# Expert stage of a two-block transformer kernel: routing keys stored in pairs, row products respread, PSUM zeroed by ScalarE

## The reference

```python
def peer_ffn(h, w_q, sub_k1, sub_k2, expert_u, expert_v):
    q = (ht @ w_q).reshape(T, 8, 256)
    s1 = q[..., :128] @ sub_k1.T ; s2 = q[..., 128:] @ sub_k2.T      # T x 8 x 128 each
    v1, i1 = top_k(s1, 16) ; v2, i2 = top_k(s2, 16)
    vals, pos = top_k((v1[..., :, None] + v2[..., None, :]).reshape(T, 8, 256), 16)
    experts = take_along_axis(i1[..., None] * 128 + i2[..., None, :], pos)    # T x 8 x 16
    gates = softmax(vals)
    a = einsum('cd,chkd->chk', x, expert_u[experts])
    w = gelu(a) * gates
    return einsum('chk,chkd->cd', w, expert_v[experts])
```

## Time and profile before

| | us |
|---|---|
| runs: median (lowest, highest of 3) | 1773.2 (1770.69, 1775.11) |
| profiled execution, span from first to last instruction | 1771.5 |
| TensorE busy | 1735.8 |
| VectorE busy | 1119.2 |
| GpSimd busy | 301.4 |
| ScalarE busy | 240.8 |

### The profile page before, as it was taken

The page is one execution under the profiler, slowest core; times in us unless marked ns, Lnnn a source line. Parts: engine busy times, 40 slices in busy tenths (PEclk is TensorE's granted clock), DMA queues, the critical chain, the costliest instruction groups (busy, mean ns, idle before and its releaser), DMA issues.

```text
span 1771.5 us, 29553 instructions
## 1 busy us (share of the span) xinstructions
PE 1735.8 (98%) x11793; PEld 1482.8 (84%) x11793; DVE 1119.2 (63%) x2415; ACT 240.8 (14%) x599; POOL 301.4 (17%) x282
## 2 busy tenths in 40 slices
PE   8999999999999899999999999999999999999996
PEld 7898576986999899999999868699955978699942
DVE  4752432898657888799533533279974763379964
ACT  1014520110414111000000011111100001011100
POOL 0010000145433444444422200000000000000000
PEclk9999999999999999999999999999999999999998
DMA  7534234499999999999999844365554435354551
GB/s 276 190 122 164 72 119 143 155 337 372 414 416 416 405 407 398 373 412 415 415 417 418 344 202 160 126 223 172 171 173 166 167 121 191 117 170 167 170 182 50
DMA packets 76609, 439.62 MB, mean 248 GB/s; under 512 B 8566, under 2 KB 8656, under 8 KB 37840
## 3 DMA queue, kind: packets, MB, share of 16 engines
q1 hardware_dynamic: 42624, 305.15, 46.4%
q0 software_dynamic: 32592, 125.92, 18.3%
q10 hardware_dynamic: 1280, 6.95, 1.0%
HBM read 432.67 MB, written 5.24 MB: 247 GB/s over the span
## 4 chain that ended last, share of the span: by engine, by line
PE 81%; DMA 9%; DVE 8%; issue 1%; ACT 1%; POOL 0%; SPq 0%; POOLq 0%; DVEq 0%
PE ps L1139 16%; PE ps L921 14%; PE ps L540 10%; DMA arena<-u_rows,sparse_pairs 7%; PE ps L584 7%; PE ps L913 7%; PE ps L1177 4%; PE ps L623 3%; PE ps L498 3%; DVE arena L1912 2%; PE ps L776 2%; PE ps L823 2%; PE ps L789 1%; PE ps L934 1%; PE ps L1008 1%
## 5 line engine op out<-in xcount | busy, mean ns | idle before, releaser
L913 PE MATMUL ps<-xT,ring 128*128 128x150 f32 x2048 | 268.4, 293 | 0.0
L921 PE MATMUL ps<-arena,ring 128*128 128x150 f32 (+1 forms) x2048 | 266.3, 292 | 0.8 <-DMA ring<-stream 0.8
L913 PEld LDWEIGHTS ps<-xT,ring 128*128 128x128 f32 x2048 | 264.4, 191 | 0.1
L921 PEld LDWEIGHTS ps<-arena,ring 128*128 128x128 f32 x2048 | 262.3, 190 | 1.5 <-issue 1.5
L540 PE MATMUL ps<-ring,arena 128*128 128x512 f32 x416 | 181.4, 592 | 0.4 <-ACT arena L1487 0.4
L2033 DVE SCALAR_TENSOR_TENSOR arena<-arena,sparse_dots 128x1024 f32<-128x1024 f32 x105 | 134.7, 1283 | 73.4 <-DMA arena<-v_rows,sparse_pairs 68.2
L2501 POOL DMA_INDIRECT arena<-v_rows,sparse_pairs x107 | 132.8, 1241 | 224.9 <-DVE arena L2033 180.4
L1912 DVE CUSTOM_DVE_ANT_0 arena<-arena 128x1024 f32<-128x1024 f32 x107 | 127.9, 1223 | 66.9 <-DMA arena<-u_rows,sparse_pairs 66.3
L2501 POOL DMA_INDIRECT arena<-u_rows,sparse_pairs x107 | 132.4, 1238 | 167.9 <-DVE sparse_dots L1912 143.7
L2464 POOL TENSOR_SCALAR stat<-stat 128x1 f32<-128x1 f32 (+2 forms) x23 | 4.4, 190 | 913.8 <-DVE stat L2205 705.7
L540 PEld LDWEIGHTS ps<-ring,arena 128*128 128x128 f32 x416 | 78.0, 190 | 93.0 <-issue 92.3
(11 more groups left out here) (341 smaller groups left out, 2244.2 us busy)
## 6 DMA issues: line engine op xcount, KB each, us to landing
ring<-stream SPq DMA_DIRECT2D x288, 1024.0 KB, 7.5
arena<-second_params POOLq DMA_DIRECT2D x6, 1024.0 KB, 5.2
arena<-kv_scratch POOLq DMA_DIRECT2D x2, 2048.0 KB, 14.2
kv_scratch<-arena ACTq DMA_DIRECT2D x2, 1024.0 KB, 10.7
arena<-held_params ACTq DMA_DIRECT2D x1, 2048.0 KB, 16.5
arena<-u_rows,sparse_pairs POOLq DMA_INDIRECT x107, 13.7
arena<-v_rows,sparse_pairs POOLq DMA_INDIRECT x107, 11.2
arena<-second_params POOLq DMA_DIRECT2D x1, 1536.0 KB, 6.5
```

Of the source, the lines that this page charges most:

```text
L913: ins = pe.matmul(ps[:, o % 2, 0:DENSE], w[:, (o % 2) * D + k * P:(o % 2) * D + (k + 1) * P], xT[:, k, 0:DENSE], start=(k == 0), stop=(k = ...
L921: ins = pe.matmul(ps[:, 4 + k // 2, c:c + DENSE], w[:, (o % 2) * D + k * P:(o % 2) * D + (k + 1) * P], H[:, n, :], start=False, stop=last, ...
```

## The change

`sel16` holds each key and gate twice, side by side, so that the one-hots read them with an innermost run of two elements in place of a step of 0; the three one-hot instructions become four, `e_same` first, with one wait between. `DOTS_TURN` goes from 74 to 70, so that the turns are spread evenly from the first group on. The zeros in PSUM are no longer written by TensorE; ScalarE copies the zero tile into the four banks after its spill of the last keys, and TensorE waits for that (`sums_zeroed`) ahead of `mixed(1)`.

```diff
--- before.py
+++ after.py
@@ -54,7 +54,7 @@
 DOTS_SUMS = (4, 4, 4, 4, 3)
 DOTS_PICK = 3
 DOTS_FIRST = 70
-DOTS_TURN = 74
+DOTS_TURN = 70
 TURNS_UP = 116
 TURNS_DOWN = 164
 GATES_AT = 22
@@ -200,7 +200,7 @@
         stat = sb("stat", [P, 96])
         exps = sb("minus_half", [P, 16])
         mark_cell = sb("mark_cell", [P, 1])
-        sel16 = sb("sel16", [P, 4, DENSE], F16)
+        sel16 = sb("sel16", [P, 4, DENSE, 2], F16)
         e1 = sb("e1", [P, 2, 2, GROUP, HEAD], F16)
         e2 = sb("e2", [P, 2, GROUP, P], F16)
         e_same = sb("e_same", [P, 2, GROUP, HEAD], F16)
@@ -401,7 +401,7 @@
         iota_ready = sem("iota_ready")
         x_wide_ready = sem("x_wide_ready")
         dot_gelu_b, weight_b_ready = sem("dot_gelu_b"), sem("weight_b_ready")
-        zeros_ready = sem("zeros_ready")
+        zeros_ready, sums_zeroed = sem("zeros_ready"), sem("sums_zeroed")
         e_ready, gates_psum, gates_applied = sem("e_ready"), sem("gates_psum"), sem("gates_applied")
         expert_psum, expert_gelu = sem("expert_psum"), sem("expert_gelu")
         xres_T_psum, xres_T_ready = sem("xres_T_psum"), sem("xres_T_ready")
@@ -974,12 +974,8 @@
             mixed(0)
 
             pe.wait_ge(xres_T_ready, 4)
-            pe.wait_ge(zeros_ready, 1)
-            pe.wait_ge(xkv_ready, 16)
+            pe.wait_ge(sums_zeroed, 4)
             pe.wait_ge(gates_applied, GROUPS)
-            for b in range(4):
-                pe.matmul(ps[:, 4 + b, :], zeros[:], zeros[:].unsqueeze(1).to_broadcast([P, 4, P]),
-                          start=True, stop=False, skip_group_check=True)
             mixed(1)
 
             def down_turn(m, turns, last=False):
@@ -1414,6 +1410,11 @@
             act.dma_start(kv_scratch[0][:, K0_FIRST * 2 * T:KT * T],
                           yT[:, 0:KT - 2 * K0_FIRST, :].rearrange("p k t -> p (k t)")).then_inc(k0b_spilled, 16)
 
+            act.wait_ge(zeros_ready, 1)
+            for b in range(4):
+                act.copy(ps[:, 4 + b, :].rearrange("p (n c) -> p n c", n=4),
+                         zeros[:].unsqueeze(1).to_broadcast([P, 4, P])).then_inc(sums_zeroed, 1)
+
             def expert_act(n, b, m):
 
                 if b == 0:
@@ -2047,8 +2048,9 @@
             for n, i in enumerate(TILES):
                 dve.wait_ge(routed_psum, n + 1)
                 w = min(P, DENSE - i * P)
-                dve.tensor_copy(sel16[:, :, i * P:i * P + w],
-                                ps[:, 2 + n, :].rearrange("p (j t) -> p j t", j=4)[:, :, 0:w]).then_inc(sel_ready, 1)
+                dve.tensor_copy(sel16[:, :, i * P:i * P + w, :],
+                                ps[:, 2 + n, :].rearrange("p (j t) -> p j t", j=4)[:, :, 0:w].unsqueeze(3)
+                                .to_broadcast([P, 4, w, 2])).then_inc(sel_ready, 1)
             dve.wait_ge(sel_ready, 2)
             dve.wait_ge(iota_ready, 1)
 
@@ -2057,17 +2059,23 @@
                 if not first:
                     dve.wait_ge(gates_psum, q - 1)
 
-                def key(j, n):
-                    return sel16[:, j, group_at(g):group_at(g) + GROUP].unsqueeze(2).to_broadcast([P, GROUP, n])
+                def two(tile):
+                    return tile.rearrange("p t (m z) -> p t m z", z=2)
+
+                def of_token(j, n):
+                    return sel16[:, j, group_at(g):group_at(g) + GROUP, :].unsqueeze(2)\
+                        .to_broadcast([P, GROUP, n // 2, 2])
 
                 def numbers(a, n):
-                    return iota16[:, a:a + n].unsqueeze(1).to_broadcast([P, GROUP, n])
-
-                dve.tensor_tensor(e2[:, b], numbers(0, P), key(1, P), ALU.is_equal)
-                link(dve.tensor_tensor(e_same[:, b], numbers(hf * HEAD, HEAD), key(0, HEAD), ALU.is_equal))
-                gates_of = sel16[:, 2:4, group_at(g):group_at(g) + GROUP].unsqueeze(3).to_broadcast([P, 2, GROUP, HEAD])
-                dve.tensor_tensor(e1[:, b], e_same[:, b].unsqueeze(1).to_broadcast([P, 2, GROUP, HEAD]), gates_of,
-                                  ALU.mult).then_inc(e_ready, 1)
+                    return iota16[:, a:a + n].rearrange("p (m z) -> p m z", z=2).unsqueeze(1)\
+                        .to_broadcast([P, GROUP, n // 2, 2])
+
+                step.inc(dve.tensor_tensor(two(e_same[:, b]), numbers(hf * HEAD, HEAD), of_token(0, HEAD), ALU.is_equal))
+                dve.tensor_tensor(two(e2[:, b]), numbers(0, P), of_token(1, P), ALU.is_equal)
+                dve.wait_ge(dve_step, step.n)
+                for part in range(2):
+                    ins = dve.tensor_tensor(two(e1[:, b, part]), two(e_same[:, b]), of_token(2 + part, HEAD), ALU.mult)
+                ins.then_inc(e_ready, 1)
 
             def apply_gates(g, q, b, hf):
```

## The result

The changed kernel takes 1765.29 us (median; 1763.68 to 1767.05, 4 runs), the kernel before beside it 1773.68 (1770.69 to 1775.11, 4 runs): a ratio of 0.9949, 95% interval 0.9935 to 0.9964, or 9 us less by the ratio and 8.4 us by the medians. The forecast was 1763.8 us. All ratios here are of fast runs; three executions far above the others of their kernel (1813 us in pairs_only, 1927 in down_171, 6466 in the kernel before) are in none of them. The profiled execution has a span of 1763.4 us and a time of 1765.17.

A forecast was written before the change was run, and what follows sets the result against it. TensorE was taken as the bound, busy 1735.8 of 1771.5 us. Savings of 4.60 + 2.43 + 3.43 less 1.0 gave 9.4 us, so 1762.1 on the span and 1763.8 on the median; likeliest range 1761 to 1766.5, wider 1760.8 to 1770.5.

The forecast's parts named there:

- The turn: DOTS_TURN 74 to 70: second one-hots ready before TensorE's second gate group; 7.03 us saved, slow clock behind the wait included.
- The stall: TensorE's idle time before the second gate group, waiting for VectorE's one-hots: 4.60 us, claimed to go whole.
- What follows the stall: Gate matmuls and next three blocks after TensorE's wait at the second gate group, slowed by half clock: 2.43 us saved.
- The zeros: Zero matmuls at 720.5 us go, 3.43 us saved; ScalarE's copies cost a 1.0 us TensorE gap near 444.7 us.
- The pairs: One-hots 2.0 us a group instead of 3.1, or 3.2 at worst; hidden behind TensorE's blocks, so counted as zero.
- The sum: Whole forecast saving: 4.60 + 2.43 + 3.43 - 1.0 = 9.4 us (9.46, cut for the rounding).
- Rival 1: Expert stage's second half: rows need 411.5 GB/s of DMA; at 402, 6.4 us is lost, leaving 3.0; chance 0.24.
- the end reserve: VectorE's wait of 14.44 us after its adds at 982.1; the same bytes 9 us earlier cost about 6.
- What follows the expert stage moves with it: After the expert stage: TensorE's own pace, so the 9.4 us saved carries to the end.
- Rival 2: Inner runs of two slow the one-hots, deciding from 3.2 us a group; at 4.6 us, 1789 us total; chance 0.03.
- Rival 3: ScalarE's zero copies cost more: stall 3 us or so, possibly half clock of 2.4; gain 5.0 or less; chance 0.07.

The follow-up runs named there:

- pairs_only: The kernel before with only the doubled sel16 and the paired one-hots: 1770.70 us, ratio 0.9985 against the kernel before.
- down_171: The changed kernel with TURNS_DOWN 171 instead of 164 (row products done by the end of the second half's groups): 1771.12 us, 0.9987 against the kernel before.
- after_turn74: The changed kernel with DOTS_TURN back at 74, pairs and ScalarE's zeros kept: 1764.34 us, ratio 0.9949 against the kernel before.
- pad1_before: The kernel before with one useless TensorE matmul on zeros ahead of the expert stage: 1770.75 us, ratio 0.9989 against the kernel before.
- zeros_only: The kernel before with only the zeros moved to ScalarE copies: 1767.47 us, ratio 0.9969 against the kernel before.
- zeros_early: The changed kernel with three of ScalarE's four zero copies moved ahead of the spill: 1765.52 us, ratio 0.9957 against the kernel before.
- pad_before: The kernel before with four useless TensorE matmuls on zeros ahead of the expert stage: 1771.09 us, ratio 0.9982 against the kernel before.
- turns_126: The changed kernel with TURNS_UP 126 instead of 116 (row products done by the end of the first half): 1776.63 us, 1.0012 against the kernel before.

## Why the prediction came out right, step by step

**The turn.** The stall and the half clock went as said, and alone the edit brings the 7.05 us of stage time that its term has. But the term belongs to three edits. The prediction counted the pairs at zero and the zeros at their matmuls because it had already removed the stall with the turn; after_turn74 shows that the other two would have removed nearly all of it (0.56 us left). The sum was right since each piece of stall was counted once, and with the turn in place the zeros bring their 2.41 us; the division of the stall among the edits was not a fact of the kernel.

**What follows the stall.** The half clock of 2.43 us went with it. Shorter waits brought shorter ones: the blocks behind it took 8.04 us for three with the zeros alone and 7.59 with the pairs alone, against 6.37.

**The zeros.** 3.43 us of matmuls went; the copies took 2.15 us (2.4 forecast, 1.9 to 3.0), the gap was 0.84 (1.0), at the third block, and the clock stayed full. A copy into PSUM took 581 to 591 ns against 592 to 628 from PSUM, but four together took 2.15 us against about 2.1; the Trainium skill's rule (ScalarE: Activation LUTs, "Step-by-step: what each stage is for") that writing to PSUM is the faster way is hardly borne out by these rows, which differ in their source as well (the zero tile is read with a step of 0).

**The pairs.** One-hots of 0.43, 0.69 and twice 0.4 us (0.42, 0.7 and twice 0.42 forecast); the copy of keys and gates 1.47 us for both (at most 1.4). By the Trainium skill (Vector Engine (DVE) Microarchitecture Reference, section 5.1) pairs would run at the double rate and elements repeated by a step of 0 at the single one. The trace agrees: with an innermost run of two the 1024-wide compare went from 1220 ns to 0.69 us and the 512-wide from 685 ns to 0.43.

**The sum.** 9.46 forecast, 9.56 measured in the expert stage. The median is 1.5 us above the forecast, about what the half clock at 90 us cost this profiled execution. In the fourteen profiled executions of this study, all with the same code up to there, six show a granted clock of 1.00 from 80 to 100 us and a stage start of 440.4 to 440.6 (443.9 with the added matmuls), five 0.91 and a start 1.4 to 1.8 us later, three 0.83 and 3.3 us later. It is no effect of the change: pad1_before, which has none of its three edits, shows it as well. Nor does the stall of the kernel before take it up: in pad1_before and zeros_only VectorE's first row product came later by as much as the stage. That the half clock is why the median lies above the forecast is argued from the one profiled execution and not shown for the others.

**Rival 1.** It did not come: 415 GB/s from 572 to 842 us, against the 411.5 needed. The cost to the end reserve was put at about 6 us, and 14.44 - 8.55 = 5.9. "What follows the expert stage moves with it" held by half a microsecond, and by luck: the prediction looked at the reserve of 14.44 us and not at the last adds, which had 0.86 us to spare before. zeros_early shows that a further gain of 0.97 us is given back at 1009 us. Rival 1's mechanism is what bounds the next step.

**Rival 2** did not come. Its limit of 3.2 us a group was about right (3.8 less 0.49 is 3.3), its price too high: above the limit the loss begins only once a lead of 5 us or more is used up. **Rival 3** did not come.

## What to carry to other kernels

Where several edits shorten one wait, run each alone and the whole with each left out (here two of the three): the gains alone (6.0, 5.5 and 2.7 us here) don't add up, and an edit that is large alone may be worth nothing beside the others. Where two streams share a full DMA, as here at 415 GB/s, holding the engine that consumes one can let the other run ahead, so a wait for the second can shrink by more than the hold (4.60 us for 3.3 held). Before the next edit, look at what ends just ahead of need behind the stage (here the row sums, by 0.5 us), and count leads as well as rates.

## What had not been expected of the hardware

Work added to TensorE, 3.3 us of it, made a kernel 3 us faster (pad_before), while the DMA gave 0.8 MB from the weights to the rows. The length of a wait alone does not say whether the half clock follows in these runs: waits of 1.90 us (zeros_only), 2.10 (pad1_before), 2.12 and 3.11 (turns_126), 3.05 (pairs_only) and 4.60 us were followed by blocks at a lower clock, waits of 2.01 and 2.27 us (down_171), 1.89 (turns_126) and 0.56 (after_turn74) were not. And a stretch in which TensorE never stops, at about 90 us, runs at full clock in some executions and partly at the half in others of the same code.
